# A head's sum of squares in one matmul over 128 rows, summed in part by GpSimd, in a two-layer encoder kernel

## What is computed

```python
def one_block(args):
    qn_b, qr_b = args
    sc = (jnp.einsum('bqhd,bkhd->bhqk', qn_b, k_nope, ...)
          + jnp.einsum('bqhr,bkr->bhqk', qr_b, k_rope, ...))
    w = jax.nn.softmax(sc * scale, axis=-1)
    return jnp.einsum('bhqk,bkhd->bqhd', w.astype(v.dtype), v)
...
mix = jnp.concatenate([group_rms_norm(attn, g_attn_out[i], N_HEADS),
                       group_rms_norm(conv, g_conv_out[i], CONV_GROUPS)], axis=-1)
x = x + rms_norm(mix @ w_out[i], g_post_mix[i])
```

## Time and profile before

| | |
|---|---|
| time of the runs, median of 3 | 2713.84 us (2713.72 to 2714.42) |
| span of the profiled execution | 2712.5 us |
| PE busy | 2698.8 us (99%) |
| DVE busy | 2034.9 us (75%) |
| ACT busy | 1398.9 us (52%) |
| POOL busy | 302.7 us (11%) |
| granted TensorE clock | 1.000 of full speed throughout |
| chain that ended last | PE 96%, DVE 2%, ACT 1% |

### The profile page before, as it was taken

One profiled execution on the slowest core, in us unless ns is written; L12 is line 12 of the kernel. 1 busy time (PEld: TensorE's weight loads), 2 busy tenths in 40 slices (PEclk: granted clock), 3 DMA queues, 4 the chain that ended last, 5 costly groups with the idle time before them and its releaser, 6 DMA issues.

```text
span 2712.5 us, 34671 instructions
## 1 busy us (share of the span) xinstructions
PE 2698.8 (99%) x12854; PEld 2242.9 (83%) x12854; DVE 2034.9 (75%) x2758; ACT 1398.9 (52%) x2401; POOL 302.7 (11%) x329
## 2 busy tenths in 40 slices
PE   9999999999999999999999999999999999999999
PEld 7888888888888888888888888888888888888886
DVE  5468888476787777798866788893867787777986
ACT  5337888564333333356634478884633333333464
POOL 0230000001111111110003200000011111111000
PEclk9999999999999999999999999999999999999999
DMA  4221112531111111133232111133311111111422
GB/s 166 78 72 37 34 34 76 181 109 71 62 47 55 39 58 51 63 117 117 86 119 73 60 41 34 29 132 131 140 45 49 63 47 55 39 55 55 148 94 78
DMA packets 85943, 206.19 MB, mean 76 GB/s; under 512 B 8976, under 2 KB 37776, under 8 KB 84752
## 3 DMA queue, kind: packets, MB, share of 16 engines
q1 hardware_dynamic: 85776, 203.97, 22.3%
HBM read 172.42 MB, written 31.52 MB: 75 GB/s over the span
## 4 chain that ended last, share of the span: by engine, by line
PE 96%; DVE 2%; ACT 1%; DMA 0%; issue 0%; SPq 0%; ACTq 0%
PE ps L1135 28%; PE ps L1137 28%; PE ps L1136 28%; PE ps L1344 4%; PE ps L1369 2%; PE ps L1368 2%; DVE nm L2386 1%; PE ps L1174 0%; PE ps L1175 0%; DVE ptl L2393 0%; PE ps L1309 0%; PE ps L1202 0%; ACT hh L1653 0%; DVE wl L2147 0%; PE ps L1160 0%; PE ps L1161 0%
## 5 line engine op out<-in xcount | busy, mean ns | idle before, releaser
L1135 PE MATMUL ps<-hh,wh 128*128 128x512 f32 x2160 | 847.9, 393 | 1.4 <-DVE hl L2183 1.3
L1137 PE MATMUL ps<-hh,wl 128*128 128x512 f32 x2160 | 840.8, 389 | 0.0
L1136 PE MATMUL ps<-hl,wh 128*128 128x512 f32 x2160 | 840.7, 389 | 0.0
L1653 ACT ACTIVATE wh<-raw 128x256 fp32r<-128x256 f32 (+2 forms) x510 | 319.2, 631 | 443.2 <-PE ps L1137 314.5
L2147 DVE TENSOR_TENSOR wl<-raw,wh 128x256 fp32r<-128x256 f32 (+2 forms) x510 | 379.6, 757 | 159.0 <-ACT wh L1653 158.6
L1135 PEld LDWEIGHTS ps<-hh,wh 128*128 128x128 f32 x2160 | 405.6, 188 | 89.1 <-issue 3.6
L1136 PEld LDWEIGHTS ps<-hl,wh 128*128 128x128 f32 x2160 | 405.6, 188 | 86.9 <-issue 3.6
L1137 PEld LDWEIGHTS ps<-hh,wl 128*128 128x128 f32 x2160 | 405.5, 188 | 84.5
L2574 DVE TENSOR_TENSOR xf<-xf,ps 128x1024 f32<-128x1024 f32 x280 | 337.4, 1214 | 35.9 <-PE ps L1137 34.7
L1135 PE MATMUL ps<-hx,wh 128*128 128x512 f32 x448 | 174.4, 389 | 0.5 <-DVE xf L2574 0.5
L1137 PE MATMUL ps<-hx,wl 128*128 128x512 f32 x448 | 174.3, 389 | 0.0
(11 more groups left out here) (241 smaller groups left out, 4303.3 us busy)
## 6 DMA issues: line engine op xcount, KB each, us to landing
raw<-w_units SPq DMA_DIRECT2D x170, 512.0 KB, 3.4
raw<-w_units SPq DMA_DIRECT2D x112, 256.0 KB, 2.9
x_mid<-xf SPq DMA_DIRECT2D x4, 2048.0 KB, 7.9
xf<-x_mid SPq DMA_DIRECT2D x4, 2048.0 KB, 7.7
hh<-mix_hi SPq DMA_DIRECT2D x14, 512.0 KB, 6.1
hl<-mix_lo SPq DMA_DIRECT2D x14, 512.0 KB, 7.0
stage<-w_head SPq DMA_DIRECT2D x16, 320.0 KB, 3.3
mix_hi<-cyh SPq DMA_DIRECT2D x8, 512.0 KB, 2.6
```

What stands on the lines that cost most here:

```text
L1135: nc.tensor.matmul(dst, ah, bh, start=start, stop=False)
L1136: nc.tensor.matmul(dst, ah, bl, start=False, stop=False)
L1137: return nc.tensor.matmul(dst, al, bh, start=False, stop=stop)
L1653: return nc.scalar.activation(dst, src, ACT.Copy, **more)
```

## The change

The two matmuls of `var` become one. The 64 rows of squares are split into a high and a low part that are put into the two halves of the 128 rows of one tile, and one matmul against all ones sums both. There is no room left for the denominator's rows, so its term is added to one row of squares first: `load_sums` loads a single row, and GpSimd adds it (`add_sums`, a 1x512 addition) between `square` and `sq_high`.

The orders change with it. On PE `var.0.0` moves behind the last values and scores of the head. On ACT `ln.0.0 r.0.0` leave the end of the head and stand in the next one as `ln.-1.0 r.-1.0`, between `high.0.0.1` and `exp.0.1`; `sq_high.0.0` goes behind `q.1.1`, and `sq_high.-1.1` behind `high.0.3.0`. On DVE `scale.-1.0` goes behind `low.0.0.1`, `sq_low.-1.1` behind `low.0.3.0` and `sq_low.0.0` behind `least.1.0`. On SP `load_sums` waits for other semaphores: a first half's for the `scale` of the half before (`o_y`) instead of its `ln` (`o_ln`), a second half's for the first half's addition (`den_add`).

```diff
 ATT_PE
-score.1.0 pv.0.2.0 turn.0.7.0 turn.0.7.1 mix.1.0 var.0.0 pv.0.2.1 score.1.1
+score.1.0 pv.0.2.0 turn.0.7.0 turn.0.7.1 mix.1.0 pv.0.2.1 score.1.1 var.0.0
 ATT_ACT
-high.0.0.0 high.0.0.1 exp.0.1 y.-1.0 v.1.0 k.1.0 last.7.1 exp.0.2 high.0.1.0 high.0.1.1 exp.0.3 v.1.1 k.1.1
-out.-1.1 high.0.2.0 high.0.2.1 square.-1.1 sq_high.-1.1 unit.0 last.6.0 high.0.3.0 high.0.3.1 exp.0.4 ln.-1.1
+high.0.0.0 high.0.0.1 ln.-1.0 r.-1.0 exp.0.1 y.-1.0 v.1.0 k.1.0 last.7.1 exp.0.2 high.0.1.0 high.0.1.1 exp.0.3 v.1.1 k.1.1
+out.-1.1 high.0.2.0 high.0.2.1 square.-1.1 unit.0 last.6.0 high.0.3.0 sq_high.-1.1 high.0.3.1 exp.0.4 ln.-1.1
...
-out.0.0 high.0.6.0 high.0.6.1 square.0.0 last.7.3 sq_high.0.0 q.1.1 high.0.7.0 high.0.7.1 exp.1.0 ln.0.0 r.0.0
+out.0.0 high.0.6.0 high.0.6.1 square.0.0 last.7.3 q.1.1 sq_high.0.0 high.0.7.0 high.0.7.1 exp.1.0
 ATT_DVE
-scale.-1.0 low.0.0.0 low.0.0.1 least.0.2 ...
-low.0.2.0 low.0.2.1 sq_low.-1.1 least.0.4 low.0.3.0 low.0.3.1 ...
+low.0.0.0 low.0.0.1 scale.-1.0 least.0.2 ...
+low.0.2.0 low.0.2.1 least.0.4 low.0.3.0 sq_low.-1.1 low.0.3.1 ...
-sum.0.0 low.0.6.0 low.0.6.1 den.0.1 last.7.3 sq_low.0.0 least.1.0 q_low.1.1 ...
+sum.0.0 low.0.6.0 low.0.6.1 den.0.1 last.7.3 least.1.0 sq_low.0.0 q_low.1.1 ...

-            return (wh[:, 1, 0:4, :], wl[:, 1, 0:4, :]) if h < HEADS - 1 else (yh[:, :], yl[:, :])
+        def square_part(h, low):
+            part = rows(h % 2 if low else 1 - h % 2)
+            return half_of(wh, 1)[part, 0, :] if h < HEADS - 1 else yh[part, :]
+        def sum_row(h, i):
+            first = V_DIM * (1 - h % 2)
+            return sq[first:first + 1, i, :]
 # load_sums
-                    if O:
-                        sp.wait_ge(o_ln, O)
-                    sp.dma_start(sq[rows(1 - h % 2), 0, :], sums[O:O + 1].partition_broadcast(V_DIM)).then_inc(den_in, 16)
+                    if t:
+                        sp.wait_ge(den_add, O)
+                    elif O:
+                        sp.wait_ge(o_y, O)
+                    sp.dma_start(sum_row(h, 1), sums[O:O + 1]).then_inc(den_in, 16)
 # variances
-                    two_passes(ps[:, 6 + t, :], ones_r[:, 2 + a, :], *square_parts(h)).then_inc(o_var, 1)
+                    parts = half_of(wh, 1)[:, 0, :] if h < HEADS - 1 else yh[:, :]
+                    nc.tensor.matmul(ps[:, 6 + t, :], ones_r[:, 0, :], parts, start=True, stop=True).then_inc(o_var, 1)
 # output_squares, high_of_squares
-                    nc.scalar.activation(sq[rows(a), 0, :], of[rows(a), :], ACT.Square).then_inc(o_sq, 1)
+                    nc.scalar.activation(sq[rows(1 - a), 0, :], of[rows(a), :], ACT.Square).then_inc(o_sq, 1)
-                    act.wait_ge(den_in, 16 * O + 16)
+                    act.wait_ge(den_add, O + 1)
-                    copy(square_parts(h)[0], sq[:, 0, :]).then_inc(o_sq_hi, 1)
+                    copy(square_part(h, 0), sq[rows(1 - h % 2), 0, :]).then_inc(o_sq_hi, 1)
 # low_of_squares
-                    low(rest, sq[:, 0, :], high).then_inc(o_sq_lo, 1)
+                    low(square_part(h, 1), sq[rows(1 - h % 2), 0, :], square_part(h, 0)).then_inc(o_sq_lo, 1)
 # GpSimd
+                def add_sums(h, t):
+                    O = (L * HEADS + h) * 2 + t
+                    pool.wait_ge(den_in, 16 * O + 16)
+                    pool.wait_ge(o_sq, O + 1)
+                    pool.wait_ge(den_sq, min(O + 2, (L + 1) * HEADS * 2))
+                    nc.gpsimd.tensor_tensor(sum_row(h, 0), sum_row(h, 0), sum_row(h, 1), ALU.add).then_inc(den_add, 1)
                 for h in range(HEADS):
                     for t in range(2):
                         O = (L * HEADS + h) * 2 + t
                         pool.wait_ge(s_exp, step(L, h, 4 * t + 3) + 1)
                         if O >= 2:
                             pool.wait_ge(den_turn, O - 1)
+                            pool.wait_ge(den_add, O - 1)
                         part = den[:, h % 2, 4 * t:4 * t + 4]
                         nc.gpsimd.tensor_tensor(den2[:, t, 0:4], part, part, ALU.mult).then_inc(den_sq, 1)
+                        if h or t:
+                            add_sums(*((h, 0) if t else (h - 1, 1)))
+                add_sums(HEADS - 1, 1)
```

More of the change, by code:

```diff
@@ L219 @@
 turn.0.4.1 score.0.7 pv.0.1.0 pv.0.1.1 turn.0.5.0 turn.0.5.1 mix.0.0 q.1.1 turn.0.6.0 turn.0.6.1 mix.0.1
-score.1.0 pv.0.2.0 turn.0.7.0 turn.0.7.1 mix.1.0 var.0.0 pv.0.2.1 score.1.1
+score.1.0 pv.0.2.0 turn.0.7.0 turn.0.7.1 mix.1.0 pv.0.2.1 score.1.1 var.0.0
 """)
 ATT_ACT = steps("""
-high.0.0.0 high.0.0.1 exp.0.1 y.-1.0 v.1.0 k.1.0 last.7.1 exp.0.2 high.0.1.0 high.0.1.1 exp.0.3 v.1.1 k.1.1
-out.-1.1 high.0.2.0 high.0.2.1 square.-1.1 sq_high.-1.1 unit.0 last.6.0 high.0.3.0 high.0.3.1 exp.0.4 ln.-1.1
+high.0.0.0 high.0.0.1 ln.-1.0 r.-1.0 exp.0.1 y.-1.0 v.1.0 k.1.0 last.7.1 exp.0.2 high.0.1.0 high.0.1.1 exp.0.3 v.1.1 k.1.1
+out.-1.1 high.0.2.0 high.0.2.1 square.-1.1 unit.0 last.6.0 high.0.3.0 sq_high.-1.1 high.0.3.1 exp.0.4 ln.-1.1
 last.7.2 exp.0.5 v_turned.1 high.0.4.0 high.0.4.1 r.-1.1 q.1.0 exp.0.6 y.-1.1 high.0.5.0 high.0.5.1 exp.0.7
-out.0.0 high.0.6.0 high.0.6.1 square.0.0 last.7.3 sq_high.0.0 q.1.1 high.0.7.0 high.0.7.1 exp.1.0 ln.0.0 r.0.0
+out.0.0 high.0.6.0 high.0.6.1 square.0.0 last.7.3 q.1.1 sq_high.0.0 high.0.7.0 high.0.7.1 exp.1.0
 """)
 ATT_DVE = steps("""
-scale.-1.0 low.0.0.0 low.0.0.1 least.0.2 k.1.0 last.7.1 least.0.3 low.0.1.0 low.0.1.1 y.-1.0 k.1.1 sum.-1.1
-low.0.2.0 low.0.2.1 sq_low.-1.1 least.0.4 low.0.3.0 low.0.3.1 den.0.0 least.0.5 unit.0 last.6.0 last.7.2
+low.0.0.0 low.0.0.1 scale.-1.0 least.0.2 k.1.0 last.7.1 least.0.3 low.0.1.0 low.0.1.1 y.-1.0 k.1.1 sum.-1.1
+low.0.2.0 low.0.2.1 least.0.4 low.0.3.0 sq_low.-1.1 low.0.3.1 den.0.0 least.0.5 unit.0 last.6.0 last.7.2
 v_turned.1 least.0.6 q.1.0 low.0.4.0 low.0.4.1 scale.-1.1 least.0.7 q_low.1.0 low.0.5.0 low.0.5.1 q.1.1
-sum.0.0 low.0.6.0 low.0.6.1 den.0.1 last.7.3 sq_low.0.0 least.1.0 q_low.1.1 low.0.7.0 low.0.7.1 y.-1.1
+sum.0.0 low.0.6.0 low.0.6.1 den.0.1 last.7.3 least.1.0 sq_low.0.0 q_low.1.1 low.0.7.0 low.0.7.1 y.-1.1
 least.1.1
@@ L684, in encoder @@
         den_in = sem("den_in")
+        den_add = sem("den_add")
         o_var = sem("o_var")
@@ L871, in low_at @@
             return yl[rows(a), :] if h < HEADS - 2 else hl[rows(a), PAIRS - 1, hs(t)]
-        def square_parts(h):
-            return (wh[:, 1, 0:4, :], wl[:, 1, 0:4, :]) if h < HEADS - 1 else (yh[:, :], yl[:, :])
+        def square_part(h, low):
[4 more added lines that the diff above has]
+            return sq[first:first + 1, i, :]
         def is_kr(w):
@@ L2411, in low_of_squares @@
                     dve.wait_ge(o_sq_hi, (L * HEADS + h) * 2 + t + 1)
-                    high, rest = square_parts(h)
-                    low(rest, sq[:, 0, :], high).then_inc(o_sq_lo, 1)
+                    low(square_part(h, 1), sq[rows(1 - h % 2), 0, :], square_part(h, 0)).then_inc(o_sq_lo, 1)
                 def output(h, a, t, j):
@@ L2680, in _ @@
                             pool.wait_ge(den_turn, O - 1)
+                            pool.wait_ge(den_add, O - 1)
                         part = den[:, h % 2, 4 * t:4 * t + 4]
                         nc.gpsimd.tensor_tensor(den2[:, t, 0:4], part, part, ALU.mult).then_inc(den_sq, 1)
+                        if h or t:
+                            add_sums(*((h, 0) if t else (h - 1, 1)))
+                add_sums(HEADS - 1, 1)
+                pool.wait_ge(den_add, (L + 1) * HEADS * 2)
                 pool.wait_ge(x_new, post_at(L, 0) * 16 + 16)
```

## The result

| | before | after |
|---|---|---|
| time of the runs, median | 2713.84 us (2713.47 to 2714.68) | 2729.11 us (2728.32 to 2729.49) |
| ratio to before, 95% interval | | 1.0054 [1.0044, 1.0065] |
| span of the profiled execution | 2712.5 us | 2727.7 us |

The changed kernel is 15.3 us slower. The forecast was 2718.2, its range ended at 2724. The sign of the likeliest case was right, the size was not.

What follows compares the result with a forecast made beforehand. PE was taken as the bound, busy 99% of the span. -7.4 (matmuls) + 7.6 (heads 1 to 6) + 2.2 (head 7) + 1.4 (GpSimd and DVE) + 0.6 (last halves) = +4.4 us: 2718.2 us, range 2708 to 2724.

Steps and rivals of the forecast that it cites:

- the likeliest case: The forecast's own case: slower, 2718.2 us, running from 2714 to 2721; chance 0.57.
- What bounds the kernel, and what is removed: PE, busy 99%, bounds; dropping `var`'s second matmul 32 times saves 0.23 us each, 7.4 us, 0.46 a head.
- ACT's order, heads 1 to 6: `ln` and `r` ahead of `exp.0.1` make `score.0.3` wait 0.63 us a head, 7.6 us in all.
- T: Start of a head's first transposes on PE, `turn.0.0`; `score.0.3` was forecast at T + 4.24 instead of T + 3.61.
- Head 7: `score.7.3` already waits there, so the new ACT order adds 1.1 us, twice 2.2 us.
- GpSimd at the head's end: Addition of 1.29 us between `square` and `sq_high`, holding up DVE's scaling: 0.1 us at each of 14 head ends, 1.4 us.
- the cover: Room left at the head's end before the new `turn.0.0` would be late: 0.2 us.
- the 0.63 behind it: The forecast wait at `score.0.3`, in which most of the 0.3 us lateness of `turn.0.0.1` was to lie.
- The last halves: Addition exposed at head 7's last half, with no later head to hide in: 0.3 us, twice 0.6 us.
- GpSimd becomes what the head's end waits for: Rival at `high.0.7`, `exp.1.0` and `low.0.7`: a longer addition costs 4 to 7 us, 2721 to 2724; chance 0.27.

Runs made afterwards that it cites:

- the mixes: Changed kernel with old places of `ln`, `r`, `scale`, `var.0.0` earlier, `den.0.1` late: 2755.58 us; SP's order mended 2717.65; further variants 2715.71, 2718.17, 2714.17.
- the short additions: Changed kernel with the last three GpSimd additions of a layer one element wide instead of 512: 2726.32 us, ratio 1.0047.
- the addition beside the chain: Changed kernel, GpSimd adding an unneeded row to itself, `sq_high` waiting for it only at a layer's last half: 2724.1 us, ratio 1.0037.

## Why the prediction was wrong, step by step

- *What bounds the kernel, and what is removed*: right. PE's waits go onto the end. The removed matmul is worth 0.44 us a head where it was forecast at 0.46. But I took all 7.4 us, also the part that falls where PE waits for others. The run with that matmul alone ended 3.8 us faster (its span 5.2). "As long as nobody is later for it" was written down and then not asked for head 7.
- *ACT's order, heads 1 to 6*: right in mechanism and nearly in size, 0.67 a head against 0.63. In part that is luck: with the orders alone `score.0.3` is late by 0.54 on average, and the 0.11 lost behind a matmul that PE waits for, which I did not have, makes up the difference. In after `score.0.3` comes at T + 4.14 and T + 4.42 in turn; 4.24 was forecast.
- *Head 7*: 2.2 us forecast for the order; all of the rest behind head 7 is 1.4 with the order alone. The error here and the one at the matmul offset each other, since both spend the same slack: together they were forecast at +2.4 and measured at +2.7. That this sum came out is luck.
- *GpSimd at the head's end*: **the step that failed.** 1.4 us stood there, 0.1 a head, and it is 8.5 us of span in the heads, 0.61 a head. The length of the addition was right (1.28 us on average, 1.29 forecast), and so was the hold-up of the scaling as an event. Three things were not. The way from the addition's end to the head's start was longer than its cover: `square` stood 0.14 later against the end of the head than before, from `least.1.0` to the first `low.0.7` on DVE went 2.56 us, 0.2 more than I had, and from the end of that `low` to `turn.0.0` another 0.15, for which I had nothing; the cover was 0.2. Second, the held-up scaling moves the *first* `low`, so `turn.0.0` itself is late by 0.5, where I had only `turn.0.0.1` late by 0.3. And third, I let most of that lateness go as lying "inside the 0.63 behind it". It can't: `score.0.3` waits for an exp that follows `ln`, `r`, the two `high` and those same transposes. When they are late the exp is later by the same. With T on time, without the addition, `score.0.3` is at T + 4.00 and T + 4.37 in turn; with T late, in after, at T + 4.14 and T + 4.42. Nothing of the lateness comes back, and 0.1 a head is added.
- One more flaw did not decide it here, but would have in the mixes: the cover was read at head 3 alone. In before the first `low.0.7` ends 0.92 us ahead of T at heads 3, 5 and 7, but 0.69 at heads 2, 4 and 6.
- The Trainium skill, page "SBUF — State Buffer", section "SBUF: two separate sides", has a GpSimd operation and a DVE operation in a two-port mode shut each other out for a whole instruction, whichever starts first. The trace agrees: at 15 of the 16 second halves the scaling begins inside the addition, takes 0.73 to 1.03 us and ends 0.04 us behind it; at the sixteenth it begins 0.04 us ahead of the addition and takes 0.18. That the scaling is in such a mode still no row says. I had given this rule 1.4 us; by it and by the queue behind it, 8.5 us came in the heads, and taking it away brought 4.7.
- *The last halves*: 0.6 us forecast for the addition there, 2.8 measured for its width alone, out of 4.0 us of span that the addition adds from head 7 on. Of the other 1.2, 0.3 a layer lie between T of head 7 and its last transposes (28.49 us with the short additions, 28.16 without any); the rest was not taken apart. In after the last `sq_high` starts 1.50 us of idle time behind its square, and `var` waits 0.74.
- *The rivals*: "GpSimd becomes what the head's end waits for" is what happened, at the place that was named. Its price of 2721 to 2724 was hung on a longer addition, up to 1.8 us; the addition was 1.28 us long, and the time came from the scaling in front of `low`. It had a chance of 0.27, too little for a cover of 0.2 us against a chain of four steps on three engines.

The sum by the runs: -3.8 (the matmul) + 6.5 (the orders on top of it) + 12.4 (the addition) = +15.1 of the 15.3 measured. Each term is the difference of two runs, so the sum closes by itself; it proves none of them.

## What to carry to other kernels

A fast engine's instruction that is saved is worth its time only where that engine is the last to be ready; read the places where it already waits, and take the saving off the list there. Cover of a few tenths of a microsecond under a chain through three engines is no cover, and a lateness does not hide in a later wait whose releaser hangs on the same late work. Two delays of which one lies under the other do not add up: after the first is removed the second shows. When a step is moved, follow its DMAs on their queue to the last user: that was missed three times here, for 28, 38 and 4 us, some of the first two through the lower clock behind PE's long waits. And see how long a stand-in instruction takes before its run is read: the addition beside the chain was 0.25 us shorter than the one that it stood for.

## What the runs showed of the hardware

An addition of one row of 512 on GpSimd costs as much as one of 128 rows: 32 of them in after, against the 1293 ns of the earlier trace rows.

```profile
L2691 POOL TENSOR_TENSOR sq<-sq 1x512 f32<-1x512 f32 x32 | 40.8, 1276 | 95.5 <-ACT sq L1905 77.7 <-issue 17.7
```

With one row read twice it takes 1.03 us, and with one element 0.18. While it runs, DVE's scaling is held, but its STREAM_TRANSPOSE of the same 128x32 (356.28, begun inside the addition) takes 0.20 us as ever.

Also, heads of the new orders alternate by 0.3 us, where most of those of before take 34.29. One head after the one shown, ACT's `ln` starts before the two `high` have ended (397.70), and `exp` follows `r` by 0.54 us instead of 0.65:

```profile
396.50 1.20 ACT L1663 ACTIVATE pth<-ps 128x512 fp32r<-128x512 f32 x2 [0.95 <-PE ps L1353]
397.59 0.58 ACT L1922 ACTIVATE sq<-ps 64x512 f32<-64x512 f32 x1
398.20 0.63 ACT L1926 ACTIVATE sq<-sq 64x512 f32<-64x512 f32 x1
398.74 1.09 ACT L1875 ACTIVATE pr<-ps,nm 128x1024 f32<-128x1024 f32 x1
```

The two differ in which 64 rows `ln` and `r` work on. That an operation overlaps the end of the one before it by 0.1 us only when both begin at the same row fits these rows, and DVE's rows above, 0.71 us from the 64-row `sq_low` to `q_low` and 0.61 from there to `low.0.7`. It was not tried by a run of its own and stays a reading.
